# The last two down units of a split-precision feed-forward, taken together one token half at a time

## The reference

```python
def swiglu(x, w_gate, w_up, w_down):
    return (jax.nn.silu(x @ w_gate) * (x @ w_up)) @ w_down

hdn = swiglu(rmsnorm_2(x, ng[0]), ffn1_w_gate[layer], ffn1_w_up[layer], ffn1_w_down[layer])
x = x + 0.5 * rmsnorm_2(hdn, ng[1])
...
hdn = swiglu(rmsnorm_2(x, ng[4]), ffn2_w_gate[layer], ffn2_w_up[layer], ffn2_w_down[layer])
x = x + 0.5 * rmsnorm_2(hdn, ng[5])
```

## Time and profile before

| | |
|---|---|
| median of 3 runs | 2092.16 us (2089.12 to 2094.69) |
| span of the profiled execution | 2090.2 us |
| PE busy | 1877.7 us, 90% of the span |
| DVE busy | 996.5 us, 48% |
| ACT busy | 584.5 us, 28% |
| DMA | 405.49 MB, mean 194 GB/s |

### The profile page before, as it was taken

The page is one execution under the profiler, slowest core; times in us unless marked ns, Lnnn a source line. Parts: engine busy times, 40 slices in busy tenths (PEclk is TensorE's granted clock), DMA queues, the critical chain, the costliest instruction groups (busy, mean ns, idle before and its releaser), DMA issues. The chain is left out here.

```text
span 2090.2 us, 33256 instructions
## 1 busy us (share of the span) xinstructions
PE 1877.7 (90%) x14452; PEld 1480.6 (71%) x14452; DVE 996.5 (48%) x1885; ACT 584.5 (28%) x858; POOL 35.7 (2%) x18
## 2 busy tenths in 40 slices
PE   6999999789998699979996899979996996759998
PEld 5544456675543499968875699979995775548997
DVE  4122243342221565532377466656656156756664
ACT  2000012220000433322234443344332221125332
POOL 0000000000000100000000100010000000101000
PEclk9689999788899899999987999999998998678999
DMA  9799960358999655413420355535540411034540
GB/s 366 285 421 425 424 273 20 127 222 344 424 425 424 248 190 192 171 35 124 177 81 13 136 192 185 182 121 188 192 172 21 171 54 65 4 141 162 182 161 21
DMA packets 58315, 405.49 MB, mean 194 GB/s; under 512 B 6400, under 2 KB 7808, under 8 KB 10544
## 3 DMA queue, kind: packets, MB, share of 16 engines
q1 hardware_dynamic: 58160, 403.25, 50.4%
HBM read 402.17 MB, written 1.05 MB: 193 GB/s over the span
## 5 line engine op out<-in xcount | busy, mean ns | idle before, releaser
L1787 PE MATMUL ps<-ffn_xh,ffn_wh 128*128 128x256 f32 x1408 | 405.8, 288 | 28.5 <-DVE ffn_xl L1902 28.5
L1788 PE MATMUL ps<-ffn_xl,ffn_wh 128*128 128x256 f32 x1408 | 404.3, 287 | 0.0
L1789 PE MATMUL ps<-ffn_xh,ffn_wl 128*128 128x256 f32 x1408 | 404.1, 287 | 0.0
L1878 DVE TENSOR_TENSOR ffn_wl<-w,ffn_wh 128x2048 fp32r<-128x2048 f32 (+1 forms) x136 | 304.3, 2238 | 15.9 <-ACT ffn_wh L1844 14.7
L1787 PEld LDWEIGHTS ps<-ffn_xh,ffn_wh 128*128 128x128 f32 x1408 | 276.4, 196 | 31.1 <-DVE ffn_wl L1878 29.5
L1788 PEld LDWEIGHTS ps<-ffn_xl,ffn_wh 128*128 128x128 f32 x1408 | 276.3, 196 | 1.6
L1789 PEld LDWEIGHTS ps<-ffn_xh,ffn_wl 128*128 128x128 f32 x1408 | 276.1, 196 | 0.0
L1844 ACT CAST ffn_wh<-w 128x2048 fp32r<-128x2048 f32 (+1 forms) x136 | 247.1, 1843 | 18.4 <-PEq L2299 8.2
L1885 DVE TENSOR_TENSOR ffn_zg<-ps,rs 128x256 f32<-128x256 f32 x88 | 37.4, 425 | 249.3 <-PE ps L1789 249.1
L1858 ACT ACTIVATE ffn_sil<-ffn_zg 128x256 f32<-128x256 f32 x88 | 36.8, 418 | 421.3 <-DVE ffn_zg L1885 421.2
L1787 PE MATMUL ps<-ffn_wh,ffn_hidh 128*128 128x512 f32 x352 | 137.5, 391 | 0.0
(11 more groups left out here) (499 smaller groups left out, 2825.6 us busy)
## 6 DMA issues: line engine op xcount, KB each, us to landing
w<-in_ffn_gu SPq DMA_DIRECT2D x88, 1024.0 KB, 4.9
w<-in_moe_gu SPq DMA_DIRECT2D x78, 1024.0 KB, 15.8
w_extra<-in_moe_gu SPq DMA_DIRECT2D x50, 1024.0 KB, 19.1
w<-in_ffn_dn SPq DMA_DIRECT2D x44, 1024.0 KB, 4.9
w_extra<-in_moe_dn SPq DMA_DIRECT2D x32, 1024.0 KB, 17.4
w<-in_moe_dn SPq DMA_DIRECT2D x32, 1024.0 KB, 19.4
w<-in_ab_xbc SPq DMA_DIRECT2D x6, 1024.0 KB, 4.7
w<-in_ab_out SPq DMA_DIRECT2D x6, 1024.0 KB, 4.9
```

The source lines that it names most:

```text
L1787: nc.tensor.matmul(out, wh, xh, start=start, stop=False)
L1788: nc.tensor.matmul(out, wh, xl, start=False, stop=False)
L1789: return nc.tensor.matmul(out, wl, xh, start=False, stop=stop)
L1878: nc.vector.tensor_tensor(low[:, s, at], S.buf(units[n])[:, at], high[:, s, at], ALU.subtract).then_inc(*w_split.one())
```

## The change

The loop over the units in PE's list no longer gives dn 10 a turn of its own. At dn 9 it now does dn 9 for token half 0, waits for dn 10's weights and hidden blocks, does dn 10 for token half 0 and signals `made`; then dn 9 and dn 10 for half 1, and signals `made` again. Before, both halves of dn 9 came first, and the wait for dn 10 behind them. The number of matmuls, what each bank gathers and the order in which it does are the same. `unit_done` is no longer signalled for dn 9; nothing waits for that one.

```diff
@@ -1820,16 +1820,23 @@
                     continue
+                if n == last:
+                    continue
                 pe.wait_ge(*w_split.at(n + 2))
                 pe.wait_ge(*hid_made.at(2 * i + 2))
                 if i == 0:
                     pe.wait_ge(*rooted.at(1))
+                if n < last - 1:
+                    for t in range(2):
+                        mm = down(i, n % parts, t)
+                    mm.then_inc(*unit_done.one())
+                    continue
                 for t in range(2):
-                    mm = down(i, n % parts, t)
-                    if n == last:
-                        mm.then_inc(*post.made.one())
-                if n < last:
-                    mm.then_inc(*unit_done.one())
+                    down(i, n % parts, t)
+                    if t == 0:
+                        pe.wait_ge(*w_split.at(last + 2))
+                        pe.wait_ge(*hid_made.at(2 * i + 4))
+                    down(i + 1, last % parts, t).then_inc(*post.made.one())
             pe.wait_ge(*up_scaled.at(FF_T))
```

## The result

The changed kernel took 2099.83 us at the median of 5 runs (2094.36 to 2104.36), the kernel before beside it 2090.82 us (5 runs, 2089.12 to 2094.69). The ratio is 1.0042, with a 95% interval of 1.0029 to 1.0056. It was timed twice more later on; all 26 runs together have a mean of 2099.2 us, and all 130 runs of the kernel before, from all comparisons, one of 2092.1 us. The difference is 7.1 us, give or take 1.6 (twice the standard error), or 0.34%; in the three comparisons taken singly it is 8.5, 6.6 and 8.4 us. So the change makes the kernel slower, by about twice the 3.2 us forecast. The median lies inside the forecast range of 2090 to 2101 us, but near its upper end.

The account below looks back on a forecast made before the run. PE, 90% busy, led the kernel; at the four feed-forward ends the start of half 1's squaring counted. Saving 3.95 us and paying 4 x 1.78 = 7.1 us gave 3.2 us slower, median 2092.16 to 2095.4 us, range 2090 to 2101.

Parts of the forecast that it names:

- What bounds the ends: At the four feed-forward ends, half 1's squaring start counts; it sat ready 0.90 us, 1.25 at the third: 3.95 us savable.
- The wait: Before dn 10 of half 0, PE stands still 1.78 us for hidden block 21, delaying everything queued: 7.1 us over four ends.
- What costs nothing: The dropped `unit_done` signal, SP's transfers and half 0's transposes (1.06 us, covered by work on half 1) add no time.
- The clock: In the new PE gap at each end, the granted clock should stay at 1.00, the gap being shorter than known lone gaps.
- The first rival: Clock falls in the new gap at most of the four ends, 1.7 us each: +10.0 us, 2102.2 us; chance 0.12.
- The second rival: No stall at dn 10 because hidden block 21 is there in time: full 3.95 us saved, 2088.2 us; chance 0.04.
- within 0.3%: Whole-kernel outcome of no change, a difference below about 0.3% (6.3 us), which cannot be told apart; chance 0.81.
- slower: Whole-kernel outcome of a slowdown beyond the 6.3 us bound; chance 0.15.

Follow-up runs that it names:

- early table load: Kernel before plus a one-column square root on ACT behind each feed-forward's last silu, loading the table while ACT waits for dn 10: 2088.57 us, again 2090.66 us.
- gap filled: Changed kernel plus seven unused matmuls on PE in the gap between dn 9 and dn 10 of half 0, ahead of the wait: 2098.62 us.
- first end only: Kernel before with the changed order in the first feed-forward alone: 2095.33 us, ratio 1.0019.
- only the wait moved: Kernel before with only the wait for dn 10's inputs moved 12 matmuls forward, order of matmuls unchanged: 2101.31 us, ratio 1.0039.
- before against itself: Unchanged kernel timed beside the kernel before, like the others: 2091.82 us against 2091.94, ratio 1.0002.
- last end only: Kernel before with the changed order in the last feed-forward alone: 2094.76 us, ratio 1.0010.
- changed, DVE's remainder first: Changed kernel with DVE forming dn 10's weight remainder before it scales gu 21's results, instead of behind: 2092.97 us, ratio 1.0006.
- early table load, tail filled: Kernel before with the early table load, plus twelve unused matmuls on PE behind each feed-forward's last transposes: 2089.91 us, ratio 0.9990.
- changed, tail filled: Changed kernel plus twelve unused matmuls on PE behind the last transposes of each feed-forward: 2095.74 us, ratio 1.0025.

## Why the prediction was right and where it was short

**What bounds the ends** held. Half 1's squaring was the point that counts, and its 0.90 us of standing ready (1.25 at the third end) is what the early table load took away: 0.88, 0.89, 1.24 and 0.89 us.

**The wait** held: four gaps, released by `ffn_hidl`, everything behind them late. The gap was forecast at 1.78 us, and half 1 is complete 1.82 to 1.87 us later. The idle time ends as forecast (the distance between the two starts is 1.97 us, less the usual 0.23 makes 1.74), but the first matmul behind the gap is followed at 0.30 us instead of 0.23, and the next at 0.24. This is the missing 0.1 us. (The 1.58 us of idle in the row are counted from the end of the last matmul and not from where the next would have started.) At the ends: 0.94, 0.99, 0.63 and 0.94, in sum 3.5 us for the 3.2 forecast; within the bounds of 2.5 to 4.7.

**What costs nothing** held: the tile times on DVE, SP's order and the transposes' cover are as they were.

**The clock** is the step that fell short. I asked only whether it would fall in the gap, and there it did not (1.00 through dn 9 and dn 10 in every trace). The first rival, a fall there at most ends, is therefore wrong, though its 2102.2 us are nearer to the measured median than my 2095.4. What I put aside as chance, that an opening may keep or lose 1.7 us of clock and that this cancels, is not chance behind the first end. Leave the filled tails aside: then all six traces whose first end is late by 0.94 us or more (three of the changed kernel, the gap filled, the first end only, only the wait moved) lost 6.8 us of clock behind it, and all three in which it is as before lost 3.4. The price was wrong too: I took lost clock for lost time. Behind the first end 3.4 us more of lost clock made the projections start 0.8 to 1.3 us later, and behind the second the changed kernel lost 6.8 us against 5.1 and its time to the next end didn't change.

The stretch from the first end to dn 9 of the second feed-forward, from the starts of the first L1743 and of dn 9:

| Traces | clock lost in 34 us | us |
|---|---|---|
| before, before against itself, last end only | 3.4 | 463.0, 462.8, 464.9 |
| changed (three), gap filled | 6.8 | 464.1, 467.3, 467.5, 463.8 |
| first end only | 6.8 | 465.5 |
| only the wait moved | 6.8 | 463.3 |
| changed, DVE's remainder first | 5.1 | 463.4 |
| before, early table load (two) | 5.1 | 462.6, 463.7 |
| early table load, tail filled | 3.4 | 462.2 |
| changed, tail filled | 3.4 | 462.2 |

The mean of the first row is 463.6, that of the six traces with 6.8 us lost 465.3: 1.7 us more, give or take 2.0, so hardly clear of the scatter. With 3.5 us at the ends that would be 5.2 of the measured 7.1 us, give or take 1.6. The two later stretches are the same in the three traces of the changed kernel and the two of before: 189.3 to 189.4 us between the second and third end, and 474.9 to 475.7 between the third and fourth.

Shown is that the fall of the clock behind the first end goes with how late the end is, that the projections start 0.8 to 1.3 us later with it, and that busy PE undoes this. What moves the fall against the end is the end itself: in the nine traces with the first end as before or later and no filled tail, the fall stands 18.7 to 19.1 us behind dn 9's first matmul, whether half 1 is squared 11.99, 12.93 or 13.86 us behind it. It isn't the idle gap, and it isn't the place of half 0's transposes. Why the fall keeps its distance to dn 9 is open. Not shown is that the mixer's opening makes up the rest of the 7.1 us. At 111 us behind the squaring three of the six traces have made good what the projections lost (0.05 us later than before, 0.12 and 0.58 us earlier), and in the other three it has grown (2.50, 3.25 and 3.45 us later). Why, and where the rest of the difference arises, is open.

**The second rival** (no stall) fell, as its condition did. DVE's remainder taken first shows nearly how it would have been: dn 10 starts 0.33 us late, half 1 is complete 0.44 us late, and the ends are 2.1 us faster than before.

**The chances.** The 2099.83 us lie in the range of 2090 to 2101. But "within 0.3%" had 0.81, and the difference is 0.34%; "slower" had 0.15. The 3.2 us were taken as the centre with only scatter around it, while some 3.6 us (7.1 less the 3.5 of the ends) were in no term of the sum. That the time still lies in the range is in part luck: the upper bound had been set for two fallen clocks of 1.7 us each and 2 us of scatter, and it took in by its size what the sum had left out. That the first comparison read 8.8 us and not 7.1 is within the scatter of single runs, whose standard deviation is mostly 3 to 4 us.

## What to carry to other kernels

Before work is moved ahead of other work, look at when its inputs arrive, not only at whether its consumer is waiting: here 0.9 us were to be had at each end and 1.8 were paid, because everything queued behind the wait waited with it. Ask also what makes the consumer slow. A table load in the chain was the whole of the 0.9 us, and moving it into idle time took it without a wait. And where a stage opens behind a stretch in which PE is nearly idle, a shift of the end by 1 us can move the fall of the granted clock against the next work. Here that made the opening's projections 0.4 to 1.3 us later, also behind ends that had become earlier; whether that is still there 100 us on has to be looked up in several traces.

## What the hardware showed beyond that

The place at which the granted clock falls behind the first end hardly moves against dn 9: 18.7 to 19.1 us behind its first matmul in nine traces of six kernels, although that matmul started between 891.6 and 900.0 us. It isn't so at every end. At the fourth the three traces of the changed kernel have the fall 4.1, 6.9 and 4.2 us behind the squaring. In the three traces whose end is earlier than before and whose tail isn't filled (early table load twice, DVE's remainder first) the fall comes 15.4 to 15.5 us behind dn 9's first matmul, and 5.1 us of clock are lost; why is open.

A load of the table for the square root took 1.28 us, and the next instruction started 1.29 to 1.30 us behind it, both in the chain and in idle time. The first matmul of 128 x 512 behind the wait lasts 0.47 us instead of 0.39, also where the gap ahead of it is full, so it isn't the idle time that makes it longer.
